# A decoder trunk on one core: the opening of the mixing stage reordered, with masks and exponentials a step ahead, a wait for each score bank, and the receptance-key products in the first five steps

## What is computed

```python
# attention group, per block of 128 queries, 8 heads in 2 groups of 4
p_c = masked_softmax(q @ k_cmp.T)            # 64 compressed blocks
imp = einsum('bqgrc,cs->bqgs', p_c, overlap) # importance of 16 blocks of 64 keys
idx = top_k(forced or future or imp, 8)      # the blocks that are selected
p_s = masked_softmax(q @ k_sel[idx].T)       # selected branch
p_w = masked_softmax(q @ k_win.T)            # window of 256 keys
o = g0 * (p_c @ v_cmp) + g1 * (p_s @ v_sel) + g2 * (p_w @ v_win)
# RWKV-7 group, after the scan
yn = groupnorm(y) * gn_w + gn_b
bonus = sum(r * k * r_k, axis=-1) * v        # receptance-key products
out = (yn + bonus) * g
```

## Time and profile before

| | before |
|---|---|
| median of three runs | 4003.78 us (3999.55 to 4007.43) |
| the profiled execution, own time | 3998.68 us |
| its span from first to last instruction | 3996.9 us |
| mean granted TensorE clock | 0.979 |
| PE busy | 3826.0 us, 96% |
| DVE, ACT, POOL busy | 2011.3, 1127.6, 1686.9 us |
| the mixing stage of layer 0, of layer 1 | from 853.0 and from 2837.0 us on, some 260 us each |

### The profile page before, as it was taken

How to read it: one execution, slowest core, us unless ns; L and a number is a source line. 1 busy time by engine, 2 the same in 40 slices (tenths; PEclk the granted TensorE clock), 3 DMA queues, 4 the chain that set the end, 5 groups by cost and what they waited for, 6 DMA issues and landing times. The chain is left out here.

```text
span 3996.9 us, 83770 instructions
## 1 busy us (share of the span) xinstructions
PE 3826.0 (96%) x34223; PEld 3498.1 (88%) x34223; DVE 2011.3 (50%) x4751; ACT 1127.6 (28%) x2486; POOL 1686.9 (42%) x2284
## 2 busy tenths in 40 slices
PE   8998999989999999999999989999899999999998
PEld 8988788866699999999999877888666999999998
DVE  6587544457545414414555874444674454144144
ACT  3154233347731000000212532333477210000002
POOL 5633222136764434434455321222367644344342
PEclk9999899999999999999999999999999999999998
DMA  4254433220032131131323554332200411411313
GB/s 131 85 166 159 124 93 86 74 98 7 13 118 71 43 120 61 43 137 41 109 89 98 157 173 107 86 87 71 96 9 11 140 54 43 138 43 51 130 39 99
DMA packets 204336, 349.63 MB, mean 87 GB/s; under 512 B 73411, under 2 KB 138051, under 8 KB 203075
## 3 DMA queue, kind: packets, MB, share of 16 engines
q1 hardware_dynamic: 203954, 344.29, 27.8%
HBM read 253.03 MB, written 95.90 MB: 87 GB/s over the span
## 5 line engine op out<-in xcount | busy, mean ns | idle before, releaser
L2614 POOL CAST wr_hi<-wr_raw 128x256 fp32r<-128x256 f32 x584 | 261.4, 448 | 895.8 <-PE ps L2650 890.3
L2616 POOL TENSOR_TENSOR wr_lo<-wr_raw,wr_hi 128x256 fp32r<-128x256 f32 x584 | 549.8, 941 | 46.7
L2650 PE MATMUL ps<-xh,wr_hi 128*128 128x384 f32 x2064 | 453.7, 328 | 0.0
L2650 PE MATMUL ps<-xh,wr_lo 128*128 128x384 f32 x2064 | 453.0, 327 | 0.0
L2650 PE MATMUL ps<-xl,wr_hi 128*128 128x384 f32 x2064 | 453.0, 327 | 0.0
L2717 ACT ACTIVATE de_c<-de_c 128x1088 f32<-128x1088 f32 (+1 forms) x44 | 49.1, 1115 | 1098.2 <-DVE de_c L2827 1098.2
L1379 POOL TENSOR_TENSOR rc_CT<-rc_AT,rc_masks 128x256 f32<-128x256 f32 x192 | 135.6, 725 | 527.8 <-DVE rc_AT L1414 410.2
L2650 PEld LDWEIGHTS ps<-xh,wr_hi 128*128 128x128 f32 x2064 | 348.9, 188 | 0.3
L2650 PEld LDWEIGHTS ps<-xl,wr_hi 128*128 128x128 f32 x2064 | 349.0, 188 | 0.0
L2650 PEld LDWEIGHTS ps<-xh,wr_lo 128*128 128x128 f32 x2064 | 348.8, 188 | 0.0
L2650 PE MATMUL ps<-de_mixh,wr_hi 128*128 128x384 f32 (+1 forms) x1440 | 318.4, 329 | 8.1 <-DVE de_mixl L2752 8.1
(11 more groups left out here) (457 smaller groups left out, 7601.9 us busy)
## 6 DMA issues: line engine op xcount, KB each, us to landing
sa_kvp<-in_cache SPq DMA_DIRECT2D x128, 256.0 KB
scr_xres<-de_x SPq DMA_DIRECT2D x56, 544.0 KB, 2.7
de_x<-scr_xres SPq DMA_DIRECT2D x56, 544.0 KB, 3.6
wr_raw<-in_w_gate SPq DMA_DIRECT2D x42, 512.0 KB, 3.6
wr_raw<-in_w_up SPq DMA_DIRECT2D x42, 512.0 KB, 3.7
rc_arbk<-scr_arbk SPq DMA_DIRECT2D x32, 512.0 KB, 4.5
wr_raw<-in_w_down SPq DMA_DIRECT2D x32, 512.0 KB, 3.6
pr_raw<-in_w_rw SPq DMA_DIRECT2D x28, 512.0 KB, 4.5
```

Of the source, the lines that this page charges most:

```text
L2614: pool.tensor_copy(hi[:, k, :], raw[:, k, :]).then_inc(w_hi, 1)
L2616: pool.tensor_tensor(lo[:, k, :], raw[:, k, :], f32(hi[:, k, :]), ALU.subtract).then_inc(w_ready, 1)
L2650: m = pe.matmul(ps[:, (bank + b) * BANK:(bank + b) * BANK + cols], w[:, k, :], x[:, k, o:o + cols], start=(k == 0 and i == 0), stop=(k == ...
```

## The change

Four edits, all in this stage. DVE's attention generator is called once before the first step (`ahead=1`), so that DVE does `mask` of item s and `scale` of item s-2 in step s, while its calls of the compressed and output strands stay where they are. ACT takes the exponentials of items 0 to 2 one step earlier. PE waits for each score bank by itself instead of once for both. And the receptance-key products leave the output strand for a strand of their own, `bonus_tensor`, called once in each step between PE's scores and its compressed strand: two tiles in each of steps 0 to 3, one in step 4.

```diff
-def blend(attention, compressed, output, first=False):
+def blend(attention, compressed, output, first=False, ahead=0, filler=None):
     done_c = done_o = 0
+    for i in range(ahead):
+        next(attention)
     for i in range(ATTENTION_STEPS):
         if first:
-            next(attention)
+            next(attention, None)
...
+        if filler:
+            next(filler, None)
         for _ in range(2 if i < 6 else 1):
...
-                if 2 * i - 1 > 0:
-                    pe.wait_ge(masked, 2 * i - 1)
                 diagonal = br == 0 and a + n == t + 1
                 for g in range(2):
+                    if 2 * i + g - 2 > 0:
+                        pe.wait_ge(masked, 2 * i + g - 2)
...
-                if 0 <= i + 3 < NI and ITEMS[i + 3][7]:
+                if i < -1 and 0 <= i + 4:
+                    exp(i + 4)
+                if 3 <= i + 3 < NI and ITEMS[i + 3][7]:
                     exp(i + 3)
...
+        def bonus_tensor(pe):
+            pe.wait_ge(rows_early_in, rows_count)
+            for i in range(TT):
+                n = tokens(i)
+                for hp in range(4):
+                    m = pe.matmul(ps[0:n, OB + 8 * i:OB + 8 * i + 8], rk[:, hp, i * P:i * P + n], rk8[:, hp, :], start=(hp == 0), stop=(hp == 3))
+                if i == TT - 1:
+                    m.then_inc(bonus_done, 1)
+                if i % 2:
+                    yield
...
         def output_tensor(pe):
             for i in range(TT + 2 + 3):
-                if i < TT:
-                    if i == 0:
-                        pe.wait_ge(rows_early_in, rows_count)
...
-            blend(attention_tensor(pe), compressed_tensor(pe), output_tensor(pe), first=True)
+            blend(attention_tensor(pe), compressed_tensor(pe), output_tensor(pe), first=True, filler=bonus_tensor(pe))
...
-            blend(attention_vector(dve), compressed_vector(dve), output_vector(dve), first=True)
+            blend(attention_vector(dve), compressed_vector(dve), output_vector(dve), first=True, ahead=1)
```

More of the change, by code:

```diff
@@ L1967 @@
 OUTPUT_FROM = LAG + 4
-def blend(attention, compressed, output, first=False):
+def blend(attention, compressed, output, first=False, ahead=0, filler=None):
     done_c = done_o = 0
+    for i in range(ahead):
+        next(attention)
     for i in range(ATTENTION_STEPS):
         if first:
-            next(attention)
-            assert not 1 <= i <= len(ITEMS) or done_c >= 7 * (T_ORDER.index(ITEMS[i - 1][0]) + 1) or ITEMS[i - 1][2]
+            next(attention, None)
+            assert not 1 <= i + ahead <= len(ITEMS) or done_c >= 7 * (T_ORDER.index(ITEMS[i + ahead - 1][0]) + 1) or ITEMS[i + ahead - 1][2]
+        if filler:
+            next(filler, None)
         for _ in range(2 if i < 6 else 1):
```

## The result

The changed kernel takes 4091.16 us (median of 6 runs, 4085.83 to 4099.9) against 3998.9 us (6 runs beside it, 3993.23 to 4007.43): a ratio of 1.0232, 95% interval 1.022 to 1.0243. The forecast was 4020 us, 4001 to 4036. The direction was right, and the loss of 92 us is more than five times the 16.6 us of the prediction's sum.

What follows compares the result with a forecast made beforehand. PE's own list was taken to bound the stage, behind an opening paced by a chain between engines. 2 x (7.3 - 8.0 + 9) = +16.6 us on the profiled 3998.68 gave 4015, 4020 us on the median's scale; range 4001 to 4036.

Steps and rivals of the forecast that it cites:

- The wait for `ga`: Steps 0 to 4: PE waits 5.8 and 5.5 us for this transfer; first block scores end 8.9 us later.
- The opening: From the stage's first scores to the third transposes: +7.3 us in each layer, bounds 5.5 and 8.9 us.
- the seven remaining tiles of products lie in PE's idle time of this stretch: Between first block scores and third transposes, products after the first two tiles fit in PE's gaps, 5.2 of 16 us.
- The reordering in the opening: Early masks and exponentials shorten first block scores to third transposes from 23.1 to 21.5 us, 1.6 us less.
- What leaves the later steps: Nine tiles of products leave steps 9 to 22: -8.0 us in each layer at most, taken whole.
- POOL's new waits: Behind the opening, POOL's `norm` comes later and PE waits: +9 us in each layer, half of at most 18.
- All six steps named: Steps 9, 11, 19, 23, 25 and 37, where a late `norm` of POOL falls on a pair and can delay PE.
- The separate banks: A wait for each score bank could take at most 5.2 us of PE's mask stops; nothing was taken.
- The last rival: All of POOL's waits behind the opening count: 2 x (8.9 - 8.0 + 18) = +38 us, 4042 us; chance 0.07.
- the low one: Range end of 4001 us: the leaving products pay for the wait, with the 5.5 us bound for the stage's start.
- the high one: Range end of 4036 us: 8.9 us for the stage's start and two thirds of POOL's waits.

Runs made afterwards that it cites:

- e1: The changed kernel with the receptance-key products back in the output strand, the other three edits kept; 4062.23 us, ratio 1.0157.
- e4: The changed kernel with 128 columns of the identity instead of 8 in each receptance-key product; 4076.81 us, ratio 1.0196.
- e6: The kernel before with only the receptance-key products moved, to steps 2 to 6 instead of 0 to 4; 4023.49 us, ratio 1.0052.
- e7: The kernel before with only the products moved, to steps 2 to 6, and 128 identity columns instead of 8 in each; 4001.23 us, ratio 1.0009.
- e11: The kernel before with all nine tiles of receptance-key products in a row in step 9; 4020.72 us, ratio 1.0049.
- e8: The changed kernel with products back in the output strand and DVE a step ahead only in steps 0 to 5; 4003.62 us, ratio 1.0008.
- e9: The kernel before with early exponentials, separate banks and, from step 6, only DVE's output strand behind the next mask; 4013.52 us, ratio 1.003.
- e10: The kernel before with early exponentials, separate banks and, from step 6, only DVE's compressed strand behind the next mask; 4059.66 us, ratio 1.0147.
- e2: The kernel before with only the receptance-key products moved to steps 0 to 4; 4025.53 us, ratio 1.0064.
- e5: The kernel before with only the score wait split, one for each bank; 3995.36 us, ratio 0.9989.
- e3: The changed kernel with products back in the output strand and POOL's attention strand a step ahead too; 4050.91 us, ratio 1.0128.

## Why the prediction was wrong

**The wait for `ga`: right.** It gave 5.8 and 5.5 us for PE's wait, and 8.9 us for the first block scores; measured are 4.77, 5.11 and 8.7. The landing took 11.8 to 12.4 us, as in the earlier trace rows. That 8.7 lies so near is partly luck: the wait and the two tiles were 1.3 us shorter than forecast, and the scores before them and the block scores behind them 0.5 us longer each, at the lower clock.

**The opening: the step that failed is "the seven remaining tiles of products lie in PE's idle time of this stretch".** It had PE's clock rise by 865 us, because in the old opening it "rose 4 to 5 us after PE's last longer pause". It stayed at half until 888. From the first block scores to the third transposes the new order was to take 21.5 us and took 32.1. The opening's +17.7 us come apart by e1 and e4: 8.8 that come back when the products have 128 columns and the clock is up (44.01 - 35.25), 6.9 for the wait for `ga` and PE's own work on the products (35.25 - 28.37), 2.1 for the reordering (28.37 - 26.29). In layer 1 they are 6.7, 8.8 and 2.1, so the first two are known to some 2 us. e6 shows that the two costs of the products overlap: with the wait gone nearly all of the loss stays, and e7 that with the clock back it goes.

The Trainium skill (TensorE: Matmul & The Clock Gate, "What's actually happening") says that activity releases the throttle. I took PE's issuing without a gap for that activity. The stretches of the changed kernel and of e11 show PE busy 2.00 of 2 us at 0.50, and e7, with other products in e6's places, 2.00 of 2 us at 1.00. So the row of products that I counted on to bring the clock up came with the lower level.

**The reordering in the opening, -1.6 us: it costs 2.1 to 2.5 us in layer 0** (e1, e8), 2.1 and 0.5 us in layer 1. It gains nothing in any of the four. I followed the mask of item 0 and the stop before item 6. What I didn't follow is that a mask one step ahead waits for scores that PE hasn't made yet, with the second tile's add and maximum behind it; the rows of e8 show that. But e9 and e10, with the early exponentials and no mask ahead in the opening, lost 2.4 and 1.9 us there (1.2 and 1.3 in layer 1) without that stop, at clocks of 0.62 and 0.64. So which of the two edits costs the 2 us stays open, and it is not far above the scatter of the openings.

**What leaves the later steps, -8.0 us: it was 2.6 to 4.9** (rests of e2 and e7 against before). PE's work does leave: 218.4 us busy in e7's rest against 225.3. Its idle time there grows from 12.8 to 14.8 us, its stops for masks from 4.3 to 5.0. The value taken, 8.0, was some 3 to 5 us too much.

**POOL's new waits, +9 us, at most 18: they cost 30 us, and this is the largest error.** The mechanism is right, DVE's compressed work between the reciprocal and POOL's `norm`, shown by e8 (loss gone) and e10 (loss whole, 29.8 of 30.5 us), while e9 leaves 4.9 us to the output strand. All six steps named stopped PE (items 6, 8, 16, 20, 22 and 34); items 28 and 42 weren't foreseen, because I looked only at the `norm` right behind a step and not at the output strand's instructions between. The size failed in three ways. I halved the 18 us because of margins "from none (at 951.36 us) to some 2 us"; the six stops took 12.9 us in e1 and 16.7 in the changed kernel, so the slack was 5 us at most. The two unforeseen ones add 5.5 us, which makes 18.4 and 22.2. And I priced the stop only. Behind most of the stops PE works on at half clock, 0.53 at 916 to 918 us. In e1's rest, against e8's, that shows as 10.8 us more busy time for the same products beside 19.8 more idle (8.4 and 19.9 in layer 1). So the lower clock is about a third of the loss and standing still two thirds.

**The separate banks, 0:** right within 0.1% (e5). The stops for masks, 3.9 us in a layer, go from before the first score product to before the second, and hardly any of it is given back.

**The rivals and the range.** The last rival, all of POOL's waits at 4042 us, had the mechanism and nearly the length of the stops (18 us); it too left out the clock, and the products' part in the opening. The ends of the range don't follow from their own words: the low one gives 2 x (5.5 - 8.0 + 0 to 4), 3999 to 4007 us, the high one 2 x (8.9 - 8.0 + 12) = +26, 4030 instead of 4036 us. With what is now measured the sum is 2 x (17.7 + 30.5 - 2.7) = +91 us, where 2.7 is e1's rest less that of the changed kernel; the sum closes because its terms are differences along one chain of kernels. Left open: why the clock fell behind a stop of 2.23 us (item 20) and not behind ones of 2.20 and 2.63 us (items 22 and 34).

## What to carry to other kernels

When one engine's strand is shifted by a step, lay its new list beside the lists of its partners that keep the old order: an instruction of POOL that waits for the later DVE result holds up the one behind it that is ready, and shifting the next engine too only moved the wait to ACT (e3). Follow its list past the first late instruction: what queues up behind it can hold back a `norm` two steps later. Price a stop of a nearly full PE at its length and about half as much again for the half-clock stretch behind it (here 18.4 us of stops came with 8 to 11 us of longer products), and do not halve it for slack that no row shows. The 8-column products were a poor filler here for a stretch in which the clock was still low: look at the granted clock after such products before you count them as free.

## What the runs showed of the hardware

In these runs PE's granted clock did not follow its busy share. In e11 it fell from 1.00 to 0.52 in the 2 us from 890, within a row of 8-column products that were issued without a gap, and PE was busy 2.00 of 2 us all the time; the row took 11.8 instead of 8.3 us. In an opening with 36 such products it averaged 0.52; with as many of 128 columns, it averaged 0.83, and the stretch was 11.8 us shorter (e6 and e7). The granted clock also fell behind stops of PE that lasted 2.2 to 3.5 us, in six of eight cases in layer 0 of the changed kernel. I had not expected that adding work to a product could shorten a kernel by 22 us.
